# More expert weights loaded ahead, in the bytes of the split buffers, with gathers, stores and last-expert work reordered

## The reference, cut to what matters

```
h  = RMSNorm(x);  P = h @ W_in                       # 1024 x 2888
yA = top-128 sparse attention (ReLU indexer), yB = pooling, yC = conv module
x  = x + concat(yA, yB, yC) @ W_out
t  = RMSNorm(x)
g_prob = softmax(t @ rg_w + rg_b); top-1 group of 4
e_logits = t @ re_w + re_b;        top-2 experts of the 4 in that group
for each of 16 experts:  act = silu(t @ w_gate) * (t @ w_up) * gate
                         y  += act @ w_down          # hidden 512
x  = x + y
```

## Time and profile before

| | |
|---|---|
| median of 3 runs | 1174.8 us (1172.47 to 1180.51) |
| profiled execution, own time | 1176.33 us |
| its span, first to last instruction | 1174.5 us |
| PE busy | 1115.5 us (95%), 12160 matmul instructions |
| DVE, ACT, POOL busy | 533.9, 298.3, 207.6 us |
| mean granted TensorE clock | 0.981 |
| DMA | 284.27 MB, mean 242 GB/s |

### The profile page before, as it was taken

One profiled execution on the slowest core, in us unless ns is written; L12 is line 12 of the kernel. 1 busy time (PEld: TensorE's weight loads), 2 busy tenths in 40 slices (PEclk: granted clock), 3 DMA queues, 4 the chain that ended last, 5 costly groups with the idle time before them and its releaser, 6 DMA issues. The chain is left out here.

```text
span 1174.5 us, 27602 instructions
## 1 busy us (share of the span) xinstructions
PE 1115.5 (95%) x12160; PEld 859.5 (73%) x12160; DVE 533.9 (45%) x1237; ACT 298.3 (25%) x572; POOL 207.6 (18%) x277
## 2 busy tenths in 40 slices
PE   8999998999899999999899999989979999999994
PEld 7866885688678778778488678747866678778972
DVE  5997997435211111110459889863452011111114
ACT  5234238422010000000332341683310000000002
POOL 4200000001322333232300000000012332233231
PEclk9999999998999999999989999999999999999997
DMA  9832211126899999999934132012269999999996
GB/s 341 270 121 82 77 33 54 55 90 222 282 398 402 403 404 404 403 402 394 260 118 123 53 100 80 19 37 73 93 248 325 406 404 402 403 403 405 403 317 172
DMA packets 88423, 284.27 MB, mean 242 GB/s; under 512 B 11888, under 2 KB 11952, under 8 KB 88288
## 3 DMA queue, kind: packets, MB, share of 16 engines
q1 hardware_dynamic: 71808, 237.60, 53.7%
q0 software_dynamic: 16480, 44.75, 11.8%
HBM read 259.23 MB, written 23.07 MB: 240 GB/s over the span
## 5 line engine op out<-in xcount | busy, mean ns | idle before, releaser
L1677 DVE SCALAR_TENSOR_TENSOR arena<-ps,gslot,arena 128x128 f32<-128x128 f32 x96 | 27.8, 345 | 425.5 <-ACT arena L1139 425.5
L777 PE MATMUL ps<-raw,arena 128*32 128x256 f32 x3264 | 206.8, 386 | 11.7 <-DVE arena L1670 9.3
L777 PEld LDWEIGHTS ps<-raw,arena 128*32 128x32 f32 x3264 | 150.0, 112 | 58.5 <-issue 22.7
L777 PE MATMUL ps<-arena 128*32 128x256 f32 x2880 | 182.9, 380 | 2.9 <-issue 0.6
L777 PEld LDWEIGHTS ps<-arena 128*32 128x32 f32 x2880 | 133.8, 110 | 40.9 <-issue 19.0
L403 PE MATMUL ps<-a_hi,w_hi 128*128 128x512 f32 (+1 forms) x304 | 121.5, 400 | 2.1 <-DVE w_lo L384 2.1
L405 PE MATMUL ps<-a_hi,w_lo 128*128 128x512 f32 (+1 forms) x304 | 118.7, 390 | 0.0
L404 PE MATMUL ps<-a_lo,w_hi 128*128 128x512 f32 (+1 forms) x304 | 118.7, 390 | 0.0
L567 POOL DMA_DIRECT2D y_rows<-arena x112 | 63.5, 586 | 302.4 <-ACT arena L1146 302.0
L1139 ACT ACTIVATE arena<-ps 128x384 f32<-128x384 f32 x32 | 15.7, 490 | 377.2 <-PE ps L777 377.2
L559 POOL DMA_INDIRECT gain<-h_rows,tab x96 | 93.5, 974 | 91.4 <-DVE gslot L1590 32.8
(11 more groups left out here) (227 smaller groups left out, 1425.5 us busy)
## 6 DMA issues: line engine op xcount, KB each, us to landing
raw<-in_w_gu SPq DMA_DIRECT2D x136, 512.0 KB
arena<-in_w_gu SPq DMA_DIRECT2D x120, 512.0 KB
arena<-in_w_dn SPq DMA_DIRECT2D x72, 512.0 KB
raw<-in_w_dn SPq DMA_DIRECT2D x56, 512.0 KB
raw<-in_w_in SPq DMA_DIRECT2D x40, 512.0 KB
y_rows<-arena POOLq DMA_DIRECT2D x112, 96.0 KB
raw<-in_w_out SPq DMA_DIRECT2D x16, 512.0 KB
y_rows<-arena POOLq DMA_DIRECT2D x11, 512.0 KB, 12.0
```

The lines of the kernel that those rows point to most:

```text
L777: mm = T.matmul(o, rows, piece[:, :, c * P:(c + 1) * P], start=b == 0, stop=b == 7)
L1677: ins = V.scalar_tensor_tensor(out=slu[:, s, :], in0=hidden(e, 1)[:, s, :], scalar=gslot[:, s, e:e + 1], in1=slu[:, s, :], op0=ALU.mult, o ...
```

## The change

A third set of slots, `deep`, holds 16 more expert pieces. It is laid over `a_hi`, `a_lo`, `w_hi` and `w_lo` (the same 64 KB of each partition) and is used once in a layer, by pieces 18 to 33, which load once `w_used` says that the output projection is done. The first 40 pieces (`FIRST`) so have a slot each; from piece 40 on the ring of 24 is used as before, counted from piece 40. `last_hot`, `last_slots` and `put_copies` move to behind experts 5 and 7, since they write `a_lo` and `a_hi`. In the gathers each of the three DMAs waits for its own transpose of the expert before, and `store(e-4)` stands between the second and the third gather of expert e. In the `Else` branch ACT does `last_y(l, 1)` ahead of `next_hi`, and DVE does `next_lo` after both `add_late`. Some semaphores are merged to make room for the four of `deep`.

```diff
+DEEP = 16
+FIRST = RING_E + DEEP
+HOT_AT = 5
+FIRST_SLOTS = (*range(RAW + 6), *range(RING_E, FIRST), *range(RAW + 6, RING_E))
...
+        with nc.sbuf_tensor("deep", [P, DEEP, 2, 512], F32) as deep:
+            pass
         a_hi = sb("a_hi", [P, DC, SEQ], F32R)
         a_lo = sb("a_lo", [P, DC, SEQ], F32R)
-        raw = sb("raw", [P, RAW, 1024])
         w_hi = sb("w_hi", [P, SPL, 1024], F32R)
         w_lo = sb("w_lo", [P, SPL, 1024], F32R)
+        raw = sb("raw", [P, RAW, 1024])
...
-            m = n % PIECES_L
-            slot = (m - PIECES_MIX) % RAW if m < PIECES_MIX else (m - PIECES_MIX) % RING_E
+            k = n % PIECES_L - PIECES_MIX
+            if k < 0:
+                slot = k % RAW
+            elif k < FIRST:
+                slot = FIRST_SLOTS[k]
+            else:
+                slot = (k - FIRST) % RING_E
...
                 load_expert_pieces(RAW, RAW + SIDE_MIX)
+                sp.wait_ge(w_used, l * PIECES_L + PIECES_MIX)
+                load_expert_pieces(RAW + SIDE_MIX, RAW + SIDE_MIX + DEEP)
                 sp.wait_ge(h2_stored, 16 * TT * (l + 1))
                 sp.wait_ge(ht_ready, 2 * DC * (l + 1))
-                load_expert_pieces(RAW + SIDE_MIX, RAW + SIDE_ROWS)
+                load_expert_pieces(RAW + SIDE_MIX + DEEP, DEEP + RAW + SIDE_ROWS)
                 sp.wait_ge(tab_set, 2 * (l + 1))
                 sp.wait_ge(ovx_set, l + 1)
-                load_expert_pieces(RAW + SIDE_ROWS, E * PIECES_E)
+                load_expert_pieces(DEEP + RAW + SIDE_ROWS, E * PIECES_E)
...
-                def gather(e):
-
-                    if l or e:
-                        pool.wait_ge(xt_set, SG * (E * l + e))
-                    for s in range(SG):
+                def gather(e, groups):
+
+                    for s in groups:
+                        if l or e:
+                            pool.wait_ge(xt_set, SG * (E * l + e - 1) + s + 1)
                         pool.indirect_dma_start(xg[:, s * QC:(s + 1) * QC], None, h2q[l],
...
                 for e in range(E):
-                    gather(e)
-                    if e >= 3:
-                        store(e - 3)
+                    gather(e, range(SG - 1))
+                    if e >= 4:
+                        store(e - 4)
+                    gather(e, (SG - 1,))
+                store(STORED - 2)
...
                     expert_down(l, e - 1)
-                    if e == 1:
+                    if e == HOT_AT + 2:
                         last_slots(l)
...
                 silu(l, 0)
-                silu(l, 1)
-                y_rows(l, 0)
-                put_copies(l)
-                for e in range(2, E):
+                for e in range(1, E):
                     silu(l, e)
                     if e < E - 1:
                         y_rows(l, e - 1)
+                    if e == HOT_AT + 2:
+                        put_copies(l)
...
                 with sc.Else():
+                    last_y(l, 1)
                     next_hi()
-                    last_y(l, 1)
...
-                for k in range(LAST):
-                    last_hot(k)
                 for e in range(E):
                     hidden_t(l, e)
                     if e + 2 < E:
                         rows_t(l, e + 2)
+                    if e == HOT_AT:
+                        ve.wait_ge(w_used, l * PIECES_L + PIECES_MIX + FIRST)
+                        for k in range(LAST):
+                            last_hot(k)
...
                 with ve.Else():
-                    next_lo()
                     last_y(l, 1)
                     for tt in range(LATE):
                         add_late(l, tt)
+                    next_lo()
```

More of the change, by code:

```diff
@@ L261, in trunk @@
         side_in = [sem(f"side_in{s}") for s in range(0, RING_E - RAW, SHARE)]
+        deep_in = [sem(f"deep_in{s}") for s in range(0, DEEP, SHARE)]
         w_hi_set, w_lo_set, w_used = sem("w_hi_set"), sem("w_lo_set"), sem("w_used")
@@ L285, in trunk @@
                              "tab_ready", "tab_set", "ovx_set"))
-        tabf_set, rep_ready = sem("tabf_set"), sem("rep_ready")
+        tabf_set = sem("tabf_set")
         h2_stored = sem("h2_stored")
@@ L308, in __init__ @@
                 self.at_lo = sem(f"at_lo{tag}")
-                self.y_set_a = sem(f"y_set_a{tag}")
-                self.y_set_v = sem(f"y_set_v{tag}")
+                self.y_set = sem(f"y_set{tag}")
                 self.y_stored = sem(f"y_stored{tag}")
@@ L336, in at_slot @@
         def at_slot(slot, w=1024):
+            if slot >= RING_E:
+                return deep[:, slot - RING_E]
             if slot >= RAW:
@@ L345, in landed @@
                 return raw_in[slot_of[n]], 16 * turn[n]
-            return side_in[(slot_of[n] - RAW) // SHARE], 16 * SHARE * turn[n]
+            if slot_of[n] < RING_E:
+                return side_in[(slot_of[n] - RAW) // SHARE], 16 * SHARE * turn[n]
+            return deep_in[(slot_of[n] - RING_E) // SHARE], 16 * SHARE * turn[n]
         def load(sp, n, src, w=1024):
@@ L376, in hi @@
             eng.wait_ge(*landed(n))
-            if k >= SPL:
+            if n >= PIECES_L and n % PIECES_L < SPL:
+                eng.wait_ge(w_used, n // PIECES_L * PIECES_L - PIECES_L + PIECES_MIX + FIRST)
+            elif k >= SPL:
                 eng.wait_ge(w_used, piece_of(k - SPL) + 1)
@@ L601, in _ @@
                                                 ).then_inc(over[l].xg_in, 16)
-                        pool.wait_ge(over[l].y_set_a, j + 1)
-                        pool.wait_ge(over[l].y_set_v, j + 1)
+                        pool.wait_ge(over[l].y_set, 2 * (j + 1))
                         for h in range(2):
@@ L750, in router @@
                         mm = T.matmul(ps[G * c:G * c + G, 5, s * G:(s + 1) * G], ident[:, s * G:(s + 1) * G], tabf[:], start=True, stop=True)
-                mm.then_inc(rep_ready, 1)
+                mm.then_inc(tab_ready, 1)
                 spin(7, 17)
@@ L859, in over_down @@
                 if j:
-                    pe.wait_ge(O.y_set_a, j)
-                    pe.wait_ge(O.y_set_v, j)
+                    pe.wait_ge(O.y_set, 2 * j)
                 for k in range(4):
@@ L1075, in _ @@
                         over_down(over[l], j)
-                    pe.wait_ge(over[l].y_set_a, EXTRA)
-                    pe.wait_ge(over[l].y_set_v, EXTRA)
+                    pe.wait_ge(over[l].y_set, 2 * EXTRA)
         @block.scalar
@@ L1179, in over_y @@
                     sc.wait_ge(O.y_stored, 32 * j)
-                A.activation(y_over[0], ps[:, 5, :], ACT.Copy, scale=gslot_over[:, j:j + 1]).then_inc(O.y_set_a, 1)
+                A.activation(y_over[0], ps[:, 5, :], ACT.Copy, scale=gslot_over[:, j:j + 1]).then_inc(O.y_set, 1)
             for l in range(DEPTH):
@@ L1583, in route @@
                 slots()
-                ve.wait_ge(tab_ready, l + 1)
+                ve.wait_ge(tab_ready, 2 * l + 1)
                 V.tensor_copy(tabf[:], ps[:, 3, 0:2 * E]).then_inc(tabf_set, 1)
                 V.tensor_copy(R["count"], ps[:, 2, TT * E:(TT + 1) * E])
-                ve.wait_ge(rep_ready, l + 1)
+                ve.wait_ge(tab_ready, 2 * l + 2)
                 here = ps[:, 5, 0:SG * 2 * E].rearrange("p (s n) -> p s n", s=SG)
@@ L1711, in over_y @@
                     ve.wait_ge(O.y_stored, 32 * j)
-                V.tensor_scalar(y_over[1], ps[:, 6, :], gslot_over[:, j:j + 1], None, ALU.mult).then_inc(O.y_set_v, 1)
+                V.tensor_scalar(y_over[1], ps[:, 6, :], gslot_over[:, j:j + 1], None, ALU.mult).then_inc(O.y_set, 1)
             link(V.memset(zeros, 0.0))
@@ L1909, in _ @@
                         over_y(O, j)
[L1910 to L1913, removed]
+                    ve.wait_ge(O.y_set, 2 * EXTRA)
+                    V.memset(ps[:].rearrange("p a n -> p (a n)"), 0.0).then_inc(O.y_set, 1)
+                    ve.wait_ge(O.y_set, 2 * EXTRA + 1)
                     ve.wait_ge(O.xg_in, 16 * (EXTRA + TT * TOPE))
```

## The result

The changed kernel takes 1170.24 us (1164.59 to 1174.56, 20 runs); the kernel before, run beside it, 1175.42 us (1171.97 to 1180.74, 20 runs). The ratio is 0.9949, with a 95% interval of 0.9938 to 0.9961: half a per cent faster. The forecast was 1180 us, a slower kernel, so the sign is wrong although the time lies in the range. The profiled execution took 1169.02 us with a span of 1167.2 us (before: 1176.33 and 1174.5), so the two traces are 7.3 us apart, 2 us more than the medians.

A forecast was written before the change was run, and what follows sets the result against it. The prediction took PE, with its holes during gathers, and not weights to set the pace. 1176.3 + 0 + 0.8 + 0 + 0 + 4.7 = 1181.8 us, 1180 us in terms of the median run; range 1160 to 1190 us.

The forecast's parts named there:

- What bounds the kernel now: Expert stage: weights are ahead of PE, and holes in PE's weight loads cost 1.06 us per expert from the third on.
- a reserve that never runs out: End of layer 0's experts: last weight pieces issued 19 us before use, so more lead buys nothing.
- Gathers and store: Experts' gathers, split by a store: PE's holes stay at 1.06 us per group, so the term is 0.
- the 28 fits: Groups of holes in PE's weight loads after gathers begin, 14 in a layer, 1.06 us each, 29.7 us in all.
- the one given 0.15: Rival at the experts' gathers: only the third gather's share of the holes goes, 1165 to 1170 us; chance 0.15.
- The row that I put against it: Evidence against the holes going: they also appear at expert 2, where the queue is empty before the gathers.
- Sixteen pieces ahead: Expert weights loaded earlier, 20.7 us of transfer moved per layer: 0 on PE's path, since nothing waits for them.
- The quiet stretch: SP's weight queue goes quiet before piece 58, which reuses piece 34's slot; 0 to -2.1 us, taken as 0.
- First gathers: First expert's gathers, with up to 22 weight pieces queued: +0.4 us in each layer, +0.8 us in all.
- The one-hot work: DVE's 1.81 us at its new place is followed by 5.31 us of idle time, so the term is 0.
- The end of layer 0: `next_lo` (4.63 us) now stands between the last y gather's landing and `add_sum`: +4.7 us, once.
- Late and doubled fits: Rivals at the gathers: late landings, 1187 to 1190 us, chance 0.07; holes twice per expert, 1210 us, chance 0.07.

The follow-up runs named there:

- e1_gathers_only: The kernel before with only the new order of gathers and store, no pieces ahead, old layer end: 1174.26 us, ratio 0.9966.
- e2_no_gather_change: The changed kernel with the old order, three gathers in a row and then the store: 1184.15 us, ratio 1.0056.
- e10_ring40: The changed kernel with gathers one by one, both layer-end edits, the ring of 40 slots reused and one-hot work behind expert 13: 1148.12 us, ratio 0.9735.
- The rotated slots: The changed kernel with the mixing pieces' ring slots shifted by four, so layer 1's first input-projection pieces need earlier-freed slots: 1170.58 us, ratio 0.9948.
- e12_ring40_only: The changed kernel with the ring of 40 slots reused up to piece 160, one-hot work at expert 13, one semaphore per four slots: 1158.58 us, ratio 0.9839.

## Why the prediction was wrong, point by point

**What bounds the kernel now: half right.** The trace's chain was read rightly: PE's holes set the pace, weights were not waited for. But "a reserve that never runs out" was wrong. I measured the lead from the issue of the last pieces to their use, 19 us. But in the changed kernel PE still waits for pieces whose last was issued 14.8 us earlier. By that, the true reserve before was some 4 us, an estimate: 19.1 us from issue to use before, less 14.8. `e1_gathers_only`, quicker by up to 1 us in each expert, used it up before the stage's end.

**Gathers and store: the failed step.** "If each gather has its part in them, they stay at 1.06 us. I take that, because the three holes look alike." They didn't stay: the term of 0 measured 10.0 us of gain in each layer up to the 15th SiLU, 20 us in all, from the 24 of the 28 fits that the change breaks up. Of the two readings that I had, the one given 0.15 (only a share goes, 1165 to 1170 us) is what happened, with more than the third gather's part: a pair leaves 0.25 us, a run of three 1.5 us (0.38 + 0.54 + 0.59) in the rows shown, a gather by itself nothing. The row that I put against it was no evidence: at expert 2 the queue is empty before the gathers, but they still are three in a row. That should have counted for the rival. The end of the stage, with stores and full DMA but no gathers, was in the earlier trace rows, and with it the fact that neither of these makes the fits. That the time falls beside that reading's 1165 to 1170 us is in part luck: two thirds of the 29.7 us went, not a third to a half, and the end of layer 0 and the waits for weights took the difference back. For the same reason it is luck that the time lies in my range.

The Trainium skill, "SBUF — State Buffer", section "SBUF: two separate sides", says that a DMA and a compute op cannot slow each other, which left 1180 us as the only result. Here the measurement decides against what I drew from it: moving POOL's gathers apart, with the same bytes, took PE's holes away. The page's rule is on the ports, and no run here shows where the holes arise.

**Sixteen pieces ahead: 0, right alone, wrong beside the step above.** The price was taken in the kernel with the holes. In the kernel that came out of the change it is 8.6 us, an estimate from the three ratios. The quiet stretch was foreseen, near 340 us; that it hands back about half of the transfers brought forward mattered only now.

**First gathers: +0.8, right.** The first matmul came 9.5 and 9.2 us after the first gather, 8.8 before in both layers: +0.7 and +0.4.

**The one-hot work: 0, right.** The expert in which PE transposes them takes about a microsecond longer than its neighbours, but it did so before too, with the same 1.09 us of matmuls:

```profile
329.64 1.09 PE L810 MATMUL ps<-cst,a_lo 128*128 128x128 f32 x8
```

In `e2_no_gather_change` the second interval falls from 18.0 to 16.8 us and the eighth rises from 16.5 to 17.9. The cost only moved; in `e10_ring40` it stands in the last interval.

**The end of layer 0: +4.7, right in its mechanism, short in its sum.** `add_sum` came 5.7 us behind the start of the last `add_late`, 1.1 before: +4.6 measured. Missing was the landing. I took it at its old distance from the last SiLU, 24.85 us; it was 29.26 us, +4.4. In all the stretch from that SiLU to `add_sum` cost 9.0 us, not 4.7. Part of this belongs to the change without any quicker PE: in `e2_no_gather_change`, whose last SiLU is at 557.1 us, the landing comes 27.3 us behind it, +2.4. The other 2 us appear only beside the quicker stage: PE is out of it 7.6 us earlier, and the transfers are not. The rotated slots show that it isn't the place of the four late pieces; in `e12_ring40_only`, whose expert pieces are issued 8 us earlier, the distance is back at 24.2 us. What holds the landing was not settled.

**Late and doubled fits: neither occurred.** A third signal was named and appeared: "It is wrong if the SiLU interval moves, or if a wait of L777 or L796 for a DMA appears." Both did.

Sum in the profile, by the table of milestones: +0.8 up to the first matmul, -8.4 for the stage, +9.0 for the end of layer 0, -0.1 up to the second layer's experts, -8.1 for their stage, -0.5 for the end: -7.3 us.

## What to carry to other kernels

Price two parts of a change together when one shortens the work that hides the other: a reserve that nobody waits for has a value as soon as the pace rises, and a quicker stage only moves the wait to the next transfer. Measure a lead from the landing of a piece to its use, not from its issue. Where an engine shows holes that no wait explains, look for bursts of issues on another engine at a fixed distance and try to space them, before you price the holes as fixed. When a cost shows up in a new place, look whether it has left an old one.

## What the runs showed of the hardware that was not expected

- Indirect gathers of POOL that start 1.3 us apart go with holes in PE's weight loads 2.5 us later; 2.4 us apart or more, with none. The holes are there at 406 GB/s, at 242 and at about 100, and the spacing may be filled with stores or with memsets. The exception is the second expert's group before, at the lower clock.
- PE's wait of 3.56 us for weights in `e1_gathers_only` was followed by 96 matmuls that took 8.12 us instead of 5.35, at a granted clock of 0.58 and 0.74.
- The same gather of rows landed 10.2 us after its issue in one kernel and 16.3 us in another, with DMA busy in both.
- In the changed kernel PE waited until 532.66 us for four pieces issued from 510.87 to 517.9 us; one semaphore counts all four. The Trainium skill, "DMA: Bandwidth & Descriptors", section "Why a DMA increments its semaphore by 16 and not by 1", says that the engines of one transfer finish independently and that only the full count means that all has landed. A wait on four pieces so ends only when the slowest engine of all four is done. The trace's number fits that, but no view here parts the engines, and no run gave each of these pieces its own semaphore.
